# Hybrid pool + S5 block on one core: the GLU products by Strassen's rule, z-gated y kept in DRAM, row sums for the gate one stage later

## What is computed

```python
y = jax.nn.gelu(y.reshape(bsz, seq, D_SSM).astype(u.dtype))
return y * jax.nn.sigmoid(y @ glu_w + glu_b)          # end of the S5 mixer (the GLU)
...
y_ssm = s5_mixer(...) * jax.nn.silu(z_ssm)
merged = (jax.nn.sigmoid(g_pool) * (y_pool @ w_branch_pool)
          + jax.nn.sigmoid(g_ssm) * (y_ssm @ w_branch_ssm))
out = merged @ w_out
return x + gate[:, None, :] * rmsnorm(out, norm_post)
```

## Time and profile before

| | |
|---|---|
| runs | 954.14 us median (952.98, 954.14, 954.31) |
| span of the profiled execution | 951.7 us, first to last instruction; the page gives no other time for it |
| TensorE matmuls | 4408, busy 930.3 us (98%) |
| DVE, ACT, POOL busy | 640.0, 347.6, 45.4 us |
| stage bp | 593.74 to 684.35 us |
| stage gl | 684.35 to 771.42 |
| stage bs | 771.42 to 858.50 |
| stage out | 858.50 to 945.58 |
| transfers | 164.60 MB, mean 173 GB/s |

### The profile page before, as it was taken

The page is one execution under the profiler, slowest core; times in us unless marked ns, Lnnn a source line. Parts: engine busy times, 40 slices in busy tenths (PEclk is TensorE's granted clock), DMA queues, the critical chain, the costliest instruction groups (busy, mean ns, idle before and its releaser), DMA issues.

```text
span 951.7 us, 11609 instructions
## 1 busy us (share of the span) xinstructions
PE 930.3 (98%) x4408; PEld 781.6 (82%) x4408; DVE 640.0 (67%) x916; ACT 347.6 (37%) x453; POOL 45.4 (5%) x82
## 2 busy tenths in 40 slices
PE   4999999999999999999999999999999999999997
PEld 4888888888888888888888888888888888888885
DVE  5988999877788887437898789665344444455232
ACT  6741353334444444434444436441022221223111
POOL 0019700000000000000000000000000000000000
PEclk9999999999999999999999999999999999999999
DMA  9843355446555444556898582597643268422222
GB/s 352 299 153 125 124 200 166 156 159 195 174 188 202 147 176 152 191 131 183 228 245 224 132 205 88 165 339 262 182 161 107 89 228 202 144 89 89 89 88 89
DMA packets 95719, 164.60 MB, mean 173 GB/s; under 512 B 38576, under 2 KB 55088, under 8 KB 95664
## 3 DMA queue, kind: packets, MB, share of 16 engines
q1 hardware_dynamic: 85872, 159.31, 52.1%
q10 hardware_dynamic: 9792, 4.56, 1.9%
HBM read 116.64 MB, written 47.19 MB: 172 GB/s over the span
## 4 chain that ended last, share of the span: by engine, by line
PE 97%; DVE 1%; ACT 1%; DMA 1%; issue 0%; ACTq 0%; DVEq 0%
PE ps L1948 49%; PE ps L2068 20%; PE ps L2190 9%; PE psb L2068 8%; PE ps L2139 2%; PE psb L2119 2%; PE psb L2128 2%; PE psa L2107 2%; PE psa L2026 1%; PE psa L1948 1%; DMA par_are<-in_a_re 1%; PE psb L2026 0%; PE psb L1976 0%; ACT gt L1028 0%; DVE mod_out L1400 0%
## 5 line engine op out<-in xcount | busy, mean ns | idle before, releaser
L1948 PE MATMUL ps<-bop,w_hi 128*128 128x512 f32 x1120 | 300.6, 390 | 0.9 <-DVE bop L1442 0.9
L1948 PEld LDWEIGHTS ps<-bop,w_hi 128*128 128x128 f32 x1120 | 209.3, 188 | 44.0 <-issue 1.1
L1948 PE MATMUL ps<-bop,w_lo 128*128 128x512 f32 x560 | 172.3, 389 | 0.0
L1948 PEld LDWEIGHTS ps<-bop,w_lo 128*128 128x128 f32 x560 | 105.1, 188 | 21.8
L1396 DVE TENSOR_TENSOR w_lo<-raw,w_hi 128x1024 fp32r<-128x1024 f32 x43 | 53.3, 1239 | 46.9 <-ACT w_hi L1014 46.7
L2068 PE MATMUL ps<-bop,r_hi 128*128 128x512 f32 x272 | 83.7, 389 | 0.0
L1014 ACT ACTIVATE w_hi<-raw 128x1024 fp32r<-128x1024 f32 x43 | 45.3, 1053 | 68.7 <-PE ps L1948 56.3
L2068 PEld LDWEIGHTS ps<-bop,r_hi 128*128 128x128 f32 x272 | 51.1, 188 | 10.6
L2068 PE MATMUL ps<-t_hi,r_hi 128*128 128x512 f32 x140 | 55.1, 393 | 0.0
L2068 PE MATMUL ps<-t_hi,r_lo 128*128 128x512 f32 x140 | 54.5, 390 | 0.0
L2068 PE MATMUL ps<-t_lo,r_hi 128*128 128x512 f32 x140 | 54.5, 389 | 0.0
(11 more groups left out here) (318 smaller groups left out, 1575.4 us busy)
## 6 DMA issues: line engine op xcount, KB each, us to landing
raw<-in_wstream SPq DMA_DIRECT2D x52, 512.0 KB, 5.1
pair_raw<-in_wstream SPq DMA_DIRECT2D x26, 512.0 KB, 4.2
ada<-in_w_ada SPq DMA_DIRECT2D x16, 512.0 KB, 11.2
x_tok<-in_x SPq DMA_DIRECT2D x8, 512.0 KB, 6.8
gs_d<-gt SPq DMA_DIRECT2D x8, 512.0 KB, 5.1
win_d<-win_new SPq DMA_DIRECT2D x8, 512.0 KB, 2.7
wout_d<-wout_new SPq DMA_DIRECT2D x8, 512.0 KB, 3.8
wout<-wout_d SPq DMA_DIRECT2D x8, 512.0 KB, 4.7
```

Of the source, the lines that this page charges most:

```text
L1948: last = mm(ps[slot(u)][:, f * HALF:f * HALF + HALF], a[:, k, :], b(k, f), start=k == order[0] and q == 0, stop=k == order[-1] and q == 2)
```

## The change

1. The 8 full products "gl" become 4 Strassen pairs (`GLU`, j = NP to NP+3; `LAST` is the last) with 7 half products each, in the ring, banks and order of the earlier pairs. Their weights come by `load_glu` in pairs. `side(j)` chooses between gt[0], rt[0] and gt[1], rt[1].
2. y is loaded in stage bp by k: tiles k and k+4 together into one of two slots; its sums (`yt_sums`) and splits are made by DVE and ACT among the bp products, those for k = 2, 3 partly after the last bp product (`late_high`, `late_low`).
3. 0.5 silu(z) y (`yz`) goes into the z buffers and from there back to DRAM (`store_yz`), and is loaded again in the next stages (`load_yz`) for the gating (`gate_of`).
4. `gate_sum` moves to the stage bs, two at each even n.
5. The weight stream's order becomes bs, bs, ga, ga, ...; the layout of the buffers changes.

The diff, cut to its core:

```diff
 for a in range(0, KT, 2):
-    USES += [("gl", a), ("gl", a + 1), ("ga", a), ("ga", a + 1)]
-USES += [("bs", n) for n in range(KT)]
-JOBS += [("gl", n) for n in range(KT)] + [("bs", n) for n in range(KT)]
+    USES += [("bs", a), ("bs", a + 1), ("ga", a), ("ga", a + 1)]
+JOBS += [("bs", n) for n in range(KT)]
...
+GLU = range(NP, NP + KT // 2)
+for j in GLU:
+    S_ORDER += [(j, P1), (j, P2)] + ([(j - 1, P4), (j - 1, P3)] if j > NP else []) + [(j, P6), (j, P5), (j, P7)]
+S_ORDER += [(LAST, P4), (LAST, P3)]
...
+            def load_zs(i):
+                if i >= 2:
+                    sp.wait_ge(yz_stored[i % 2], 16 * (i // 2))
+                sp.dma_start(zs_t[i % 2][:, :], zs_d[ZS_ORDER[i]]).then_inc(zs_in[i % 2], 16)
+
+            def store_yz(i):
+                sp.wait_ge(yz_done, i + 1)
+                sp.dma_start(zs_d[ZS_ORDER[i]], zs_t[i % 2][:, :]).then_inc(yz_stored[i % 2], 16)
...
+            for i in range(2):
+                load_y(i)
+                load_zs(i)
+            for n in range(KT - 1):
                 sp.wait_ge(job_out[slot(("bp", n))], evicted(("bp", n)))
+                if n == KT - 2:
+                    for s in range(2):
+                        sp.wait_ge(raw_free[s], USE["bs", 0] // 2)
+                    load_glu(NP)
+                    sp.wait_ge(yz_stored[1], 16 * 4)
+                load_gp(n + 1)
+                if n + 4 < KT:
+                    load_w(p + n + 4)
                 sp.dma_start(m1_d[n], rt[n % 2][:, :]).then_inc(m1_stored[n % 2], 16)
+                if 2 <= n < 6:
+                    k = n - 2
+                    store_yz(2 * k)
+                    store_yz(2 * k + 1)
+                    if k < 2:
...
+                        load_y(k + 2)
+                    if k < 3:
+                        load_zs(2 * k + 2)
+                        load_zs(2 * k + 3)
+            sp.wait_ge(mm_done, JOB["bp", 7] + 1)
+            load_glu(NP + 1)
...
             for n in range(KT):
+                if n % 2 == 0 and n:
+                    load_w(USE["ga", n])
+                    load_w(USE["ga", n + 1])
+                    if n + 2 < KT:
+                        load_w(USE["bs", n + 2])
+                        load_w(USE["bs", n + 3])
...
                 sp.wait_ge(m_lo_done, n + 1)
                 if n + 2 < KT:
                     sp.dma_start(rt[n % 2][:, :], m1_d[n + 2]).then_inc(reload_in[n % 2], 16)
                     sp.dma_start(gt[n % 2][:, :], gs_d[n + 2]).then_inc(g_in[n % 2], 16)
...
+            for n in range(KT - 1):
+                split_lo(USE["bp", n + 1])
                 if n == 0:
                     scans(KT - 1)
                     rotate_out(KT - 1)
+                if 2 <= n < 6:
+                    k = n - 2
+                    if k < 2:
+                        dve.wait_ge(y_loaded[k], 32)
+                        yt_sums(k)
+                    y_low(k)
+                    yz(2 * k)
+                    yz(2 * k + 1)
+                    if k < 2:
+                        yt_low(k)
+                    else:
+                        yt_sums(k)
                 m1_out(n)
...
+            j = LAST
+            c22(j - 1)
+            pair_low(j, P5)
+            pair_low(j, P3)
+            c11(j)
+            gated_low(0)
+            gated_low(1)
+            sum3(j)
+            pair_low(j, P7)
+            c12(j - 1)
+            pair_low(j, P4)
+            gate_of(5)
+            gate_of(4)
+            split_lo(USE["bs", 0])
+            for n in range(2, 6):
+                gated_low(n)
+            c22(j)
+            gate_of(7)
+            gated_low(7)
+            c12(j)
+            gate_of(6)
+            gated_low(6)
+            split_lo(USE["bs", 1])
...
             for n in range(KT):
+                if n % 2 == 0:
+                    gate_sum(n)
+                    gate_sum(n + 1)
...
                 if n < KT - 2:
-                    split_lo(USE["bs", n] + 2)
+                    split_lo(USE["bs", n + 2])
                 merge(n)
```

More of the change, by code:

```diff
@@ L438, in build @@
         gp_in, zs_in, zp_in = sem("gp_in"), two("zs_in"), sem("zp_in")
-        gated, yz_done = sem("gated"), sem("yz_done")
+        gated, yz_done, yz_stored = sem("gated"), sem("yz_done"), two("yz_stored")
         g_in = two("g_in")
@@ new lines, in _ @@
+            sp.wait_ge(mm_done, JOB["bp", 7] + 1)
+            load_glu(NP + 1)
+            for s in range(2):
+                sp.wait_ge(yz_stored[s], 16 * 4)
+            for n in range(4):
+                load_yz(n)
+            sp.dma_start(silu_row[:, :], c_d).then_inc(c_in, 16)
+            sp.wait_ge(job_out[slot(("bp", 7))], evicted(("bp", 7)))
+            sp.dma_start(m1_d[KT - 1], rt[1][:, :]).then_inc(m1_stored[1], 16)
+            pair_read(NP)
+            load_glu(NP + 2)
+            for n in (4, 5):
+                load_yz(n)
@@ new lines, in yt_high, with late_high @@
+            def yt_high(k):
+                act.wait_ge(t_made, 16 + 4 * k + 4)
+                fn(yt[:, :, k, 0, :], yt_f[:, :, k, 1, :], ACT.Copy).then_inc(t_hi_done, 1)
+            def late_high(k, s):
+                act.wait_ge(mm_done, JOB["bp", 7] + 1)
+                act.wait_ge(t_made, 16 + 4 * k + 4)
+                fn(yt_hi[:, k - 2, s, :, :], y_slot[:, k - 2, s, :, :], ACT.Copy).then_inc(t_hi_done, 1)
+            for k in range(4):
+                split_hi(USE["bp", k + 3])
+                y_high(k)
+                if k < 2:
+                    yt_high(k)
@@ new lines, in _ @@
+            pair_high(j, P5)
+            late_high(2, 0)
+            late_high(3, 0)
+            pair_high(j, P7)
+            pair_high(j + 1, P1)
+            pair_high(j + 1, P2)
+            copy_u2(j)
+            pair_high(j, P4)
+            pair_high(j, P3)
+            copy_p5(j)
+            pair_high(j + 1, P6)
+            for j in (NP + 1, NP + 2):
+                early = j == NP + 2
+                pair_high(j, P5)
+                pair_high(j, P3)
+                func_c22(j - 1)
+                copy_p1(j)
+                if not early:
+                    pair_high(j + 1, P1)
+                    pair_high(j + 1, P2)
+                c21(j - 1)
+                pair_high(j, P7)
+                pair_high(j, P4)
+                func_c11_c12(j - 1)
+                copy_u2(j)
+                if early:
+                    pair_high(j + 1, P1)
+                copy_p5(j)
+                if early:
+                    pair_high(j + 1, P2)
+                pair_high(j + 1, P6)
@@ L1337, in _ @@
[L1337 to L1341, removed]
-                evac(("gl", n), gt[n % 2][:, :], ACT.Tanh, scale=0.5, bias=glub[:, n:n + 1])
-                split_hi(USE[("gl", n + 2) if n + 2 < KT else ("bs", n + 2 - KT)])
-                act.wait_ge(gated, n + 1)
-                fn(hb(0, n), halves(y_raw[:, n, :]), ACT.Copy).then_inc(in_hi_done, 1)
+            func_c22(j)
@@ new lines, in _ @@
+            pair_low(j, P3)
+            sum1(j + 1)
+            sum2(j + 1)
+            sum4(j + 1)
+            pair_low(j + 1, P6)
+            for j in (NP + 1, NP + 2):
+                early = j == NP + 2
+                n = 2 * (j - 1 - NP)
+                c22(j - 1)
+                pair_low(j, P5)
+                pair_low(j, P3)
+                c11(j)
+                if not early:
+                    pair_low(j + 1, P1)
+                    pair_low(j + 1, P2)
+                sum3(j)
+                pair_low(j, P7)
+                c12(j - 1)
+                pair_low(j, P4)
+                gate_of(n + 1)
+                gate_of(n)
+                if early:
+                    pair_low(j + 1, P1)
+                sum1(j + 1)
+                sum2(j + 1)
+                sum4(j + 1)
+                if early:
+                    pair_low(j + 1, P2)
+                pair_low(j + 1, P6)
@@ L1956, in begin, with product @@
                     pe.wait_ge(job_out[slot(u)], evicted(u) - 1)
-            def product(u, xs, split=None, between=None):
+            def product(u, xs, split=None, between=None, order=range(KT)):
                 begin(u)
-                for k in range(KT):
+                for e, k in enumerate(order):
                     if between is not None and k == 6:
@@ L1964, in product @@
                     if split is not None:
-                        pe.wait_ge(in_lo_done, split + k + 1)
-                    last = k_step(u, k, *xs)
+                        pe.wait_ge(in_lo_done, split + e + 1)
+                    last = k_step(u, k, *xs, order)
                 last.then_inc(mm_done, 1)
```

439 lines of the change are left out of this document (308 added, 131 removed).

## The result

Changed kernel 984.1 us (median of 982.27, 983.78, 984.42 and 985.84), kernel before 953.8 in the same comparison: ratio 1.0316, interval 1.0304 to 1.0329. **Slower by 30 us.** The forecast was 974.1 with a range of 958 to 985: the sign and the places were right, the amount was 10 us short. The median lies only 0.9 us inside the range, and one of the four runs outside it: that the range held is in part luck. The profiled execution has a span of 980.4 us, 28.7 longer than that of before.

What follows compares the result with a forecast made beforehand. TensorE, busy 98% of 951.7 us, was taken as the bound. Matmuls -10.9, bp +18.3, clock +1.7, GLU +2.3, bs and out +8.6 make +20.0 on 954.1: 974.1 us, range 958 to 985.

Steps and rivals of the forecast that it cites:

- Matmuls, -10.9: Stage gl: four pairs of seven half products at 2.72 us replace 87.07 us of full products, 10.9 us less.
- bp, 18.3 + 1.7 forecast: Stage bp: TensorE waits 4.0, 9.4 and 4.9 us before bp5, bp6, bp7, plus 1.7 for a slow-clock restart.
- The loop: Stage bp: m1_out waits behind yz, yz for z, z for SyncE, SyncE for the previous m1_out; 18.3 us.
- I take 622.4, as SyncE's y loads are earlier after the change: Start of round 1 in bp: ACT begins splitting w of bp3 at 622.4, so m1_out(2) ends at 635.0.
- three more at 1.25: bp round 1: three transfers beyond today's six, at 1.25 us each, lengthen 11.2 us to 15.0.
- GLU, 2.3: Stage GLU: first pair 0.3 us late, and the last P4 waits 2.0 us for c22 behind DVE's queue.
- bs and out, 8.6 forecast: Row sums hold the weight buffers: bs4 0.2 us late, bs6 2.4, out0 3.5, its splits 2.5 more.
- 805.05 + 5.6: Stage bs, loop before bs4: the row tile's load, issued at 805.05, was taken to need 5.6 us.
- the prediction's own 24.4: Stage bs: loop before bs6 takes 9.5 + 14.9 = 24.4 us against two products of 21.76; bs6 put 2.4 late.
- (b): Rival: the merge stage bs hides its loop, +11.4 us in all, 965.5 us; chance 0.12.
- (d): Rival: z loads in bp do not queue, second z within 11.0 us of m1_out(2); -5.8, 948 us; chance 0.12.
- (c): Rival: slower transfers, 1.46 us each, 23 us in bp and 11.7 in bs and out; +29, 983 us; chance 0.10.

Runs made afterwards that it cites:

- the experiment above: One more 512 KB load in each of three bp rounds, ahead of the stores of z, added to the changed kernel (984.1 us): 989.44 us.
- the last kernel: Kernel with all three repairs and row sums behind the merge (950.62 us), its w_out loads now issued two at each of n = 0 to 3: 945.85 us.

## Why the prediction was right, and where it fell short

**Matmuls, -10.9.** Right: 48 fewer, at 2.72 us per half product, 5.44 for 24.

**bp, 18.3 + 1.7 forecast, 25.7 measured.** The loop is the one described, and opening it on VectorE takes all of it away. Its size was short by 5.7 (25.7 for 20.0), in these steps. (1) "I take 622.4, as SyncE's y loads are earlier after the change": `m1_out(2)` ended at 637.2, not 635.0. ScalarE's split did begin at 622.44, but the step overlooked that g_pool of bp1 is now issued behind the six loads of y and z; `m1_out(1)` waited for it until 624.7 (the 9.67 us at the head of the chain). A moved load was counted for what it brings and not for what it is put ahead of: **2.2**. (2) The rounds, from one `m1_out` to the next, were 20.1, 21.3 and 17.5 us long against 19.6, 20.3 and 15.8: **3.2**. The second of the two z products began 15.5, 15.6 and 12.2 us after the round's start for 15.0, 15.0 and 10.5. "three more at 1.25" is thus a little too cheap (1.4 each would give 15.5), and the transfer added in the experiment above cost still more, 1.5 to 2.7 per round. In round 2 another 0.4 passed between the second product and the sums. Most is missing in round 3, where the store landed 7.9 after the round's start and the load took 4.3, for 7.2 and 3.3. (3) Clock: bp7 12.74 - 10.88 = 1.86 for 1.7; bp5 and bp6 slow, and hidden, as stated. The Trainium skill (TensorE: Matmul & The Clock Gate, HAM oscillation) has an engine that waits for transfers in each round restart at half rate in each; the 2.08 us rows behind all three waits agree.

**GLU, 2.3.** 0.5 at the first pair for 0.3, 1.86 before P4 for 2.0; the queue in front of c22 was the cause.

**bs and out, 8.6 forecast, 11.3 measured.** Right that the hold on the weight buffers does it: the last kernel makes the same eight sums without it and has no wait there. bs4 was put at 0.2 late and was 2.04: the row tile landed 7.69 us after its issue where "805.05 + 5.6" had been taken, 2.1 more, and the weights behind it 3.12 for 3.7. bs6: 1.86 for 2.4 (the prediction's own 24.4 less 21.76 is 2.6). out0 and its splits: 4.2 + 0.6 of idle for 3.5 + 2.5. These are 8.8 in all, so the sum of the waits was right, though one by one they were not. What is missing is first the slow clock in out0: a wait of 4.21 us lowered it, and 30 matmuls cost 1.7 more. The other 0.8 is 0.16 behind each of the four waits and 0.1 for the first matmuls of bs4 and of bs6. The clock was charged once, in bp, and not at the other long wait of my own forecast.

**The rivals.** (b), merge stage hidden, and (d), faster, are out: VectorE waited for z three times and TensorE in bs; the second z was there about 15.5 us after `m1_out(2)`, not within the 11.0 that (d) asks for. (c), slower transfers at 983, gave the time best, in part by luck, for it knew nothing of the late start of 2.2 us; but its 1.46 us per transfer fits round 1 as well (11.2 + 3 x 1.46 = 15.6). What does not hold is its reason, a low rate throughout. GB/s from 637 to 653 in the changed kernel, in slices of 0.4 us:

```profile
GB/s 0 0 51 113 225 379 420 184 143 102 174 266 338 369 410 440 420 430 410 399 348 410 430 410 420 410 430 389 430 410 358 358 338 389 379 399 205 51 0 0
```

The rate is low at first (102 to 184 between 639.8 and 641.4, while SyncE is still issuing the burst) and 338 to 440 from 642.2 on. The rows above have 380 to 420 GB/s for 19 us on end in the kernel with the sums behind the merge. The Trainium skill (DMA: Bandwidth & Descriptors, Where 436 GB/s comes from) has about 358 as the HBM side's limit per core, one stack's bandwidth shared by two cores; this kernel runs on one core, for which that was no ceiling, and the measurement decides. What was dear was that a buffer's store had to land before the next load into it could be issued, 7.4 + 4.8 us, with other transfers ahead of both.

## What to carry to other kernels

When a round trip to DRAM is put beside a busy TensorE, draw the circle: which instruction waits for the load, who stands behind it on that engine, and what lets the load be issued. If the circle passes through something that TensorE needs, its whole latency counts, even where the transfer engines are busy only 0.59 of the time as here; put what TensorE needs ahead of the waiting instruction: here the same transfers then cost nothing in bp. A burst of loads that nobody needs yet is also a place in a queue, and moving one wait away shows the next.

## What I had not expected

A transfer of 512 KB ahead of the critical one costs 1.8 us (5.3 over three), of which about 0.5 is SyncE's own time to issue it (three more took it 0.48 us each); the price from bandwidth alone, 512 KB at 413 GB/s, is 1.27. And a wait of 4.21 us lowers TensorE's clock for the first matmuls of out0 while one of 2.04 before bs4 hardly does (1.17 us for four matmuls instead of 1.07). Between the two lie 2.26 and 2.51 us before bs2 in two of the experiments, after which the first four took 1.99 and 2.04.
